# Softplus of the stick-breaking units through the absolute value: one clip off VectorE, one Abs on ScalarE, and the output copies handed over

## The reference, cut to what matters

```python
logits = q @ k^T * scale
log_beta = log_sigmoid(logits)
log_keep = where(strict, log_sigmoid(-logits), 0)      # = -softplus(logits)
log_tail = reversed_cumsum(log_keep) - log_keep
weights  = where(strict, exp(log_beta + log_tail), 0)
out      = weights @ v
```

## Time and profile before

| | |
|---|---|
| median of three runs | 1801.53 us |
| the profiled execution's own time | 1801.65 us |
| its span (first to last instruction) | 1799.9 us |
| TensorE busy | 1768.3 us, 98% |
| VectorE busy | 1095.4 us, 61% |
| ScalarE busy | 732.8 us, 41% |
| granted TensorE clock | 1.00 in all stretches that were read |

### The profile page before, as it was taken

The page is one execution under the profiler, slowest core; times in us unless marked ns, Lnnn a source line. Parts: engine busy times, 40 slices in busy tenths (PEclk is TensorE's granted clock), DMA queues, the critical chain, the costliest instruction groups (busy, mean ns, idle before and its releaser), DMA issues.

```text
span 1799.9 us, 22457 instructions
## 1 busy us (share of the span) xinstructions
PE 1768.3 (98%) x8312; PEld 1428.0 (79%) x8312; DVE 1095.4 (61%) x1598; ACT 732.8 (41%) x1030; POOL 40.6 (2%) x78
## 2 busy tenths in 40 slices
PE   7999999999999999999999999999999999999998
PEld 6887556888888888878888888889766888888887
DVE  6878775655556335775677674245577667677423
ACT  7313663333444223444344443233365434444322
POOL 4110000000000000000000000000000000000000
PEclk9999999999999999999999999999999999999999
DMA  9794203232222323312322222323401232222231
GB/s 347 263 339 140 76 25 108 76 106 96 93 93 87 110 83 98 113 48 94 117 94 93 93 93 84 109 83 109 168 24 48 78 110 93 93 93 93 96 104 70
DMA packets 149081, 195.29 MB, mean 108 GB/s; under 512 B 3646, under 2 KB 133000, under 8 KB 146332
## 3 DMA queue, kind: packets, MB, share of 16 engines
q1 hardware_dynamic: 141272, 155.28, 26.5%
q0 software_dynamic: 7600, 39.13, 5.9%
q10 hardware_dynamic: 148, 0.05, 0.0%
HBM read 189.15 MB, written 5.29 MB: 108 GB/s over the span
## 4 chain that ended last, share of the span: by engine, by line
PE 91%; DVE 5%; DMA 2%; ACT 1%; issue 1%; SPq 0%; ACTq 0%; DVEq 0%
PE bank L807 20%; PE bank L809 20%; PE bank L808 20%; PE bank L870 3%; PE bank L872 3%; PE bank L871 3%; PE bank L1476 2%; PE bank L1477 2%; PE bank L1478 2%; PE bank L954 2%; PE bank L1006 1%; PE bank L975 1%; PE bank L850 1%; PE bank L851 1%; PE bank L852 1%; PE bank L1139 1%
## 5 line engine op out<-in xcount | busy, mean ns | idle before, releaser
L1947 DVE TENSOR_TENSOR w_lo<-w_stage,w_hi 128x2048 fp32r<-128x2048 f32 (+3 forms) x136 | 299.0, 2198 | 436.7 <-ACT w_hi L1504 436.5
L807 PE MATMUL bank<-act_hi,w_hi 128*128 128x512 f32 x1216 | 475.2, 391 | 1.2 <-DVE act_lo L2011 0.6
L809 PE MATMUL bank<-act_hi,w_lo 128*128 128x512 f32 x1216 | 473.2, 389 | 0.0
L808 PE MATMUL bank<-act_lo,w_hi 128*128 128x512 f32 x1216 | 473.1, 389 | 0.0
L1504 ACT ACTIVATE w_hi<-w_stage 128x2048 fp32r<-128x2048 f32 (+3 forms) x138 | 253.6, 1837 | 465.8 <-PE bank L809 335.6
L807 PEld LDWEIGHTS bank<-act_hi,w_hi 128*128 128x128 f32 x1216 | 228.3, 188 | 50.9 <-DVE act_lo L2011 2.1
L808 PEld LDWEIGHTS bank<-act_lo,w_hi 128*128 128x128 f32 x1216 | 228.3, 188 | 47.4 <-issue 0.5
L809 PEld LDWEIGHTS bank<-act_hi,w_lo 128*128 128x128 f32 x1216 | 228.3, 188 | 47.4
L807 PE MATMUL bank<-mid_hi,w_hi 128*128 128x512 f32 x352 | 136.9, 389 | 0.0
L808 PE MATMUL bank<-mid_lo,w_hi 128*128 128x512 f32 x352 | 136.9, 389 | 0.0
L809 PE MATMUL bank<-mid_hi,w_lo 128*128 128x512 f32 x352 | 136.9, 389 | 0.0
(11 more groups left out here) (412 smaller groups left out, 2621.0 us busy)
## 6 DMA issues: line engine op xcount, KB each, us to landing
ada_stage<-in_w_ada POOLq DMA_DIRECT2D x24, 1024.0 KB, 7.5
w_stage<-in_w_up SPq DMA_DIRECT2D x22, 1024.0 KB, 5.1
w_stage<-in_a_ffn_in SPq DMA_DIRECT2D x22, 1024.0 KB, 5.0
w_stage<-in_b_ffn_in SPq DMA_DIRECT2D x22, 1024.0 KB, 5.1
w_stage<-in_w_in SPq DMA_DIRECT2D x10, 1024.0 KB, 7.1
w_stage<-in_b_ffn_out SPq DMA_DIRECT2D x10, 1024.0 KB, 5.0
w_stage<-in_w_down SPq DMA_DIRECT2D x8, 1024.0 KB, 5.2
w_stage<-in_a_ffn_out SPq DMA_DIRECT2D x8, 1024.0 KB, 5.2
```

The lines of the kernel that those rows point to most:

```text
L807: pe.matmul(dst, wh, mh, start=start and k == 0, stop=False)
L808: pe.matmul(dst, wh, ml, start=False, stop=False)
L809: last = pe.matmul(dst, wl, mh, start=False, stop=stop and k == nk - 1)
L1947: dve.tensor_tensor(w_lo[slot][:, 0:n], raw[:, 0:n], w_hi[slot][:, 0:n].bitcast(FP32), ALU.subtract).then_inc(w_ready, 1)
```

## The change

Softplus is now formed as max(x, 0) + log(1 + exp(-|x|)). ScalarE takes |x| from PSUM into `tmp` (`sb_size`), Exp has scale -1 in place of 1, VectorE's clip is gone, and `sb_larger` becomes a scalar_tensor_tensor: max of the PSUM logit with 0, plus the log. `sb_save` moves from ScalarE to VectorE, at the same values of u. The clip that stood ahead of `sb_larger` for r = 3 is gone, so that `sb_larger` has one place.

```diff
-            def softplus(t, clamped, exped, logged, n):
+            def softplus(t, clamped, exped, logged, n, sign=1.0):
                 act.wait_ge(clamped, n)
-                act.activation(t, t, ACT.Exp).then_inc(exped, 1)
+                act.activation(t, t, ACT.Exp, scale=sign).then_inc(exped, 1)
...
-            def sb_save(p):
-                act.wait_ge(sb_out, p + 1)
-                act.activation(o_raw[1][:, p, :], bank[SB_OUT], ACT.Copy).then_inc(sb_saved, 1)
+            def sb_size(u):
+                act.wait_ge(sb_scores, u + 1)
+                if u == 0:
+                    act.wait_ge(sq_added, ADD0["oa"] + 2)
+                if u >= 2:
+                    act.wait_ge(sb_plus, u - 1)
+                act.activation(sb_abs(u), sb_psum(u), ACT.Abs).then_inc(sb_sized, 1)
...
                 if u < SB_UNITS:
-                    softplus(sb_clip(u), sb_clamped, sb_exped, sb_logged, u + 1)
+                    sb_size(u)
+                    softplus(sb_abs(u), sb_sized, sb_exped, sb_logged, u + 1, -1.0)
...
-                if u in (5, 9, 13):
-                    sb_save(u // 4 - 1)
...
-            sb_save(3)
             square_b(3)
...
-                dve.tensor_tensor(sb_pl[:, u % 3, :, q0:SEQ], sb_psum(u), sb_clip(u), ALU.max)\
-                    .then_inc(sb_plus, 1)
+                dve.scalar_tensor_tensor(out=sb_pl[:, u % 3, :, q0:SEQ], in0=sb_psum(u), scalar=0.0,
+                                         in1=sb_abs(u), op0=ALU.max, op1=ALU.add).then_inc(sb_plus, 1)
+            def sb_save(p):
+                dve.wait_ge(sb_out, p + 1)
+                dve.tensor_copy(o_raw[1][:, p, :], bank[SB_OUT]).then_inc(sb_saved, 1)
...
             for u in range(SB_UNITS + 1):
-                if u and u % 4 != 3:
+                if u:
                     sb_larger(u - 1)
-                if u < SB_UNITS:
-                    if u == 0:
-                        dve.wait_ge(sq_added, ADD0["oa"] + 2)
-                    if u == 2:
-                        mem_save(1, 1).then_inc(mem_saved, 1)
-                    dve.wait_ge(sb_scores, u + 1)
-                    dve.tensor_scalar(sb_clip(u), sb_psum(u), CLAMP, None, ALU.min).then_inc(sb_clamped, 1)
-                if u % 4 == 3:
-                    sb_larger(u - 1)
+                if u == 2:
+                    mem_save(1, 1).then_inc(mem_saved, 1)
                 if u and (u - 1) % 4 in (1, 2):
                     sb_add(u - 1)
+                if u in (5, 9, 13):
+                    sb_save(u // 4 - 1)
...
+            sb_save(3)
             add_squares("ob", 3)
```

More of the change, by code:

```diff
@@ L395, in program @@
         mem_q_saved = sem("mem_q_saved")
-        sb_scores, sb_clamped, sb_exped, sb_logged, sb_plus = (
-            sem("sb_scores"), sem("sb_clamped"), sem("sb_exped"), sem("sb_logged"), sem("sb_plus"))
+        sb_scores, sb_sized, sb_exped, sb_logged, sb_plus = (
+            sem("sb_scores"), sem("sb_sized"), sem("sb_exped"), sem("sb_logged"), sem("sb_plus"))
         sb_tail, sb_weights, sb_out, sb_saved, sb_added = (
@@ L747, in program, with sb_abs @@
         SB_OUT = 6
-        def sb_clip(u):
+        def sb_abs(u):
             return tmp[:, 2 * (u % 2):2 * (u % 2) + 2, sb_unit(u)[2]:SEQ]
```

## The result

The changed kernel takes 1815.55 us (median of 4 runs, 1813.60 to 1818.02), the kernel before beside it 1801.68 (1801.35 to 1802.77): ratio 1.0074, 95% interval 1.0062 to 1.0086, so 13.9 us slower. The forecast was 1811.6 with a range to 1814.5: the sign was right, and the waits it forecast are there, but the time lies above the range. The profiled execution took 1815.39 with a span of 1813.7, 13.8 more than before.

What follows compares the result with a forecast made beforehand. TensorE was taken to bound the stage, with at most 4.0 us of waits to gain. First units 2.2, two pairs 4.6, pair 3 2.7 and restarts 0.6 sum to 10.1 us slower: 1811.6 us, range 1803.0 to 1814.5.

Steps and rivals of the forecast that it cites:

- (a): First four units: four added Abs on nearly pauseless ScalarE make the tail sum of unit 3 late, +2.2 us.
- (b): Pairs 1 and 2: VectorE's copy waits for the values ahead of the larger; TensorE waits 2.22 us before unit 5's tail sum.
- (c): Old gap ahead of unit 6: clip gone, so the larger is ready in time, -1.04 us.
- (d): New gap ahead of unit 7: ScalarE's chain 5.04 us against TensorE's other work 3.92, so a wait of 1.12 us.
- (e): Pair 3: waits of 3.17 us at unit 13 and 1.23 ahead of 15, old 1.68 ahead of 14 gone; +2.7 us.
- (f): Restarts: tail sums starting from standing have a first matmul 0.15 us longer, one more per pair and one first; +0.6 us.
- (g): Last output copy, between the end of the values and the sum of squares: covered by 0.9 us, costs nothing.
- rival 4: Clock falls to 1.2 of 2.4 GHz after the long gap ahead of unit 13; no time but "above the range"; 3%.
- The share of the copy: About 5.3 us of the 10.1 hang on the copy's place on VectorE; the rest is ScalarE's longer chain.
- rival 2: Copy on VectorE costs nothing, only ScalarE's part counts: 2.0 us slower, 1803.5; 8%.
- Rival 1: Gaps ahead of tail sums of units 2, 6, 10, 14 close and nothing opens: 4.0 us gained, 1797.5; 6%.
- rival 3: Abs isn't in ScalarE's loaded table, so each Abs stands between two loads: 41 us, about 1850; 3%.

Runs made afterwards that it cites:

- e1b_fill: Changed kernel plus extra TensorE matmuls nobody reads: 6 ahead of unit 4's scores, 8 ahead of tail sums of units 5 and 9, 12 ahead of 13; 1811.81 us.
- e4_only_save: Kernel before the change, with only the output copy moved from ScalarE to VectorE, clip and Exp kept; 1812.75 us, ratio 1.0056.
- e2_late_save: Changed kernel with VectorE's output copy moved behind the larger of units 5, 9 and 13, one loop turn later; 1804.31 us, ratio 1.0013.
- e7_no_abs_old_place: Changed kernel with neither clip nor Abs (no overflow guard), output copy at the change's place; 1811.20 us, ratio 1.0047.
- e5_abs_first_r3: e2_late_save with, on ScalarE, the Abs of units with r = 3 put ahead of the weight of two units before; 1802.77 us, ratio 1.0006.

## Why the prediction was right and wrong

- **(a), the first four units, +2.2:** right. The gap ahead of unit 2 grew by 1.35 (0.25 to 1.60), and in e1b_fill, with the clock up, the tail sum of unit 3 starts 8.79 us after the start of unit 3's scores (233.31 - 224.52), before 6.71: +2.1. In the changed kernel itself its own gap can't be seen: the slow matmuls ran in its place.
- **(b), the copy's queue, 2.22 twice:** right; 2.20 twice.
- **(c), the old gaps, -1.04:** right; gone.
- **(d), the new gap ahead of units 7 and 11, 1.12:** measured 1.34. ScalarE's side was right, 5.00 from the start of the weight (247.63) to the tail sum (252.63). TensorE's side was taken 0.22 too long: I took it from rows in which unit 6 itself had waited (1.56, in running order 1.51) and the starts lay apart for that wait.
- **(e), 3.17 and 1.23:** measured 3.20 and 1.49; TensorE's work beside the second was again taken too long.
- **(f), restarts, +0.6:** wrong. The tail sum of unit 9 takes 1.13 after standing 2.20 us, as that of unit 5 before without a wait, and that of r = 2 takes 1.56 after a wait and 1.51 without, 0.05 more. The 0.15 of the prediction came from setting a row of the timeline (1.56) against rows of the chain (1.06 and 1.77), which counts the same matmuls shorter; the timeline has 1.13 and 1.94 for them. The 0.6 made up by chance for (d) and (e), 0.7 too small.
- **(g)**: right, nothing came of the last copy.
- **The clock, rival 4, is the step that failed.** I gave it 3% and no price, since no row had the lower level. It had a price: 4.9 us of slow matmuls, of which 4.1 lengthened the stage. Without them the stage is 10.4 us longer than before (71.51 - 61.13), and 10.1 were forecast; that the median of e1b_fill, 1811.81, comes within 0.2 of the forecast's 1811.6 is in part luck, since the errors of (d), (e) and (f) cancel and the chip is another. The chance was also misjudged: I looked at the longest new gap alone, while the stage had seven gaps, and the clock fell after 1.60, after 2.20 and after 3.20 us.
- **The share of the copy** was told wrong: "about 5.3 us of the 10.1". By its own words, (b) and its like in (e) less the old gaps, it would be 2 x (2.22 - 1.04) + 3.17 - 1.68 = 3.9. But the old gaps close without the copy too; by the prediction's rival 2 the copy's place is worth 10.1 - 2.0 = 8.1 of them, and measured it is more: 1815.55 against 1804.31, 11.2 us (across chips), and 10.6 alone in e4_only_save. Of the 11.2, 7.8 are waits (13.4 - 5.6); the rest is the clock: two of its three falls lie behind the copy's gaps.
- Rival 1 fell, and rival 2 with it; rival 3 too: no table load more, and Abs takes 0.38, 0.58, 0.80, 1.02, at or under the prices taken. The Trainium skill ("ScalarE: Activation LUTs", "Table sets: the hidden batching unit") has abs in every set, and the trace agrees: from 215 us to the end of the stage there are four loads before the change and four after.
- The Trainium skill's rule to keep simple work on VectorE ("ScalarE: Activation LUTs", "Rules for kernel authors") points the right way here, but not by the price of the instruction: for 512 float32 elements from PSUM the Abs took 0.58 on ScalarE and the clip 0.68 on VectorE, and yet the Abs costs the kernel 4 to 6 us, since it stands in a chain on ScalarE that VectorE's clip ran beside.

## What to carry to other kernels

An instruction that has to wait belongs behind those that are ready and that TensorE needs next. The copy waits for the values; in front of the larger of unit 5 it held up the tail sum that TensorE does next, and its place cost 11 of 14 us. There is little room on the other side: the copy frees bank 6 for the scores of unit 7, and in e2_late_save it ends at 241.50 us where those scores start at 241.75. When a change opens gaps on TensorE in a stage, price the clock beside them: work out the gaps, and then add 1.6 to 1.7 us for some of them, as nearly every fall read here cost. And whoever takes an instruction out of one queue or moves it to another must look at what stands next in every queue: here the gaps ahead of units 6, 10 and 14 closed, the one ahead of unit 2 grew, and six others opened.

## What was not expected of the hardware

- The granted clock fell after waits of 1.60 (unit 2 of the changed kernel) and 1.68 us (unit 14 of e4_only_save, which the wait of 3.20 us ahead of unit 13 precedes), but not after waits of 1.68 (unit 14 of before), 2.20 (unit 9 of the changed kernel) and 3.20 us (unit 13 of e4_only_save). The length of one gap doesn't tell it. What decides stays open.
- A fall cost 1.6 to 1.7 us of longer matmuls, but for the last of e7_no_abs_old_place, which cost 2.9.
- It shows in the spread between runs: in e7_no_abs_old_place and e5_abs_first_r3 the runs with the lower mean clock are the slower ones (1803.4 to 1805.6 at 0.997 against 1801.5 to 1802.8 above it in e5_abs_first_r3). It isn't all of the spread: in 21 runs the kernel before went from 1800.7 to 1804.7 at mean clocks of 0.998 and 0.999.
- A 128x128x128 float32 matmul with constants took 0.23 to 0.24 us in a row of its own (24 of them 5.62 us, 16 of them 3.84), shown as two records each; I had read 0.12 from a record.
